# HGRN: the first growth of the keys moved from VectorE to GpSimd

## The chip, the cores and the metric
One core of a Trainium2 chip runs the whole kernel in one launch. The metric is the time of the device in microseconds (us). TensorE multiplies, VectorE and ScalarE do the elementwise work on both memories (SBUF and the accumulators in PSUM), GpSimd does elementwise work on SBUF, and SyncE starts the DMAs.

## What is computed
The reference is one layer of a decoder, for a prompt of 512 tokens and eight samples of 8 tokens (576 tokens in all) with a model width of 1024, followed by a final RMSNorm. One projection feeds a sliding window attention and HGRN2, a recurrence of 8 heads with a 128x128 state each. Cut to that recurrence:

```python
def step(S, inp):
    qc, kc, vc, gc = inp
    b = jnp.cumsum(gc, axis=1)
    o_inter = jnp.einsum('bthk,bhkv->bthv', qc * jnp.exp(b), S)
    diff = b[:, :, None] - b[:, None, :]
    decay = jnp.where(tri, jnp.exp(jnp.where(tri, diff, 0.0)), 0.0)
    att = jnp.einsum('bthk,bshk,btshk->bhts', qc, kc, decay)
    o_intra = jnp.einsum('bhts,bshv->bthv', att, vc)
    b_last = b[:, -1]
    S = jnp.exp(b_last)[..., None] * S + jnp.einsum(
        'bshk,bshv->bhkv', kc * jnp.exp(b_last[:, None] - b), vc)
    return S, o_inter + o_intra
```

The decay between two tokens of a head is a product over the tokens between them, different for each of the 128 channels.

## The kernel before
Activations lie with the features on the 128 partitions and the 576 tokens along the columns. The big products run over weight units of 1 MB: a DMA brings a unit to `raw`, ScalarE copies it to `wR` (L1071), VectorE subtracts to get the rest that the copy lost (L1388, four instructions of 512 columns for a unit), and TensorE multiplies both parts (L832). Each engine has its own program. All of them follow one list of events, which the function `walk()` writes out, so the order of each engine's work is fixed. Into the tiles of the projection, between 318 and 600 us, `walk()` weaves the slots of HGRN: `hgrn_slots()` gives, for each head r (0 to 7) and each of the six levels l of `LEVELS = (0, 4, 8, 16, 32, 64)`, one event `g_level`, and beside it what remains of the head before (`g_keys`, `g_state`, `g_sample`, `g_out`, `g_norm`, `g_scale`) and what prepares the head after (`g_diff`, `g_exp`, `g_operands`).

The decayed scores of a head are built from small blocks to large ones. `g_exp` makes the decays inside each block of four tokens: `eD` holds the growth for each token and, in its last 144 columns, the one at the head of each block. `g_operands` makes the queries `qe` and the keys `ke` of the base level. At level 0 TensorE multiplies `ke` and `qe` (L934 and L935) and signals `s_lv`. VectorE then grows both operands, so that they hold the decay to the borders of the block of four, keeps the whole block's decay in `g`, clears `att`, and copies the scores into it under a mask (L1585, L1586). At a level l above 0 TensorE multiplies the grown operands (L941, and L944 for the samples), and VectorE grows the halves of each pair of blocks (L1572, L1573), multiplies neighbouring decays (L1574) and copies under a mask (L1590). The growth at level 0 is:

```python
if l == 0:
    head, tail = eD[:, TOK:].unsqueeze(2), blocks(eD, 4, TOK)[:, :, 3:4]
    done(dve.tensor_tensor(blocks(k, 4, TOK), blocks(k, 4, TOK), tail.to_broadcast([P, QUADS, 4]), ALU.mult))
    done(dve.tensor_tensor(blocks(q, 4, TOK), blocks(q, 4, TOK), head.to_broadcast([P, QUADS, 4]), ALU.mult))
    done(dve.tensor_tensor(G[r % 2][:, 0:QUADS].unsqueeze(2), head, tail, ALU.mult), signal)
```

These are L1564 (keys), L1565 (queries) and L1566 (the decay of the block). `done` raises a semaphore at the end of an instruction and makes the engine wait for it, so that an engine's instructions follow one another. L941 of level 1 waits for `s_op`, which L1566 raises, and for `s_pred`, which the masked copy L1586 raises. ScalarE's `g_exp` of the next head overwrites `eD`, and so waits for the `s_op` that L1566 of the head before raised.

GpSimd does only single subtractions and additions of 576 columns elsewhere: `hR` (L1710) and `rb` (L1696, L1704) around the norms, and `actR` (L1717) in the MLP. In the stage of HGRN it has no work.

Of the kernel before, what the change touches and what calls it, by code (L numbers as in the profile page):

```python
# [27 lines left out]
ALU = mybir.AluOpType  # L28
# [3 lines left out]
P = 128  # L32
# [5 lines left out]
TOK = SEQ + SMP  # L38
# [13 lines left out]
NL = len(LEVELS)  # L52
MASK = (NL - 1) * HALF + TOK
QUADS = TOK // 4
# [322 lines left out]
def program(nc, a, o):  # L377
# [5 lines left out]
    with ctx:  # L383
# [3 lines left out]
        def sem(name):  # L387
            return ctx.enter_context(nc.semaphore(name))
# [61 lines left out]
        QE, KE, ATT, G = [qe0, qe1], [ke0, ke1], [att0, att1], [g0, g1]  # L450
# [41 lines left out]
        s_pn, s_pt, s_ptc, s_pv, s_otc = (sem(n) for n in ("s_pn", "s_pt", "s_ptc", "s_pv", "s_otc"))  # L492
        s_kw = sem("s_kw")
        s_D, s_E, s_base, s_op, s_lv, s_pred = (sem(n) for n in ("s_D", "s_E", "s_base", "s_op", "s_lv", "s_pred"))
        s_hats = sem("s_hats")
        s_kt, s_ktc, s_ds, s_st, s_vb = sem("s_kt"), sem("s_ktc"), sem("s_ds"), sem("s_st"), sem("s_vb")
        s_dss, s_sn = sem("s_dss"), sem("s_sn")
        s_sic = sem("s_sic")
# [8 lines left out]
        def ordered(eng, own, start=None):  # L507

            seen = dict(start or {})

            def done(ins, s=None, by=1):
                s = own if s is None else s
                seen[s] = seen.get(s, 0) + by
                ins.then_inc(s, by)
                eng.wait_ge(s, seen[s])
            return done
# [5 lines left out]
        def square(k):  # L522

            return tmp[k % 4] if k else rb
# [26 lines left out]
        def blocks(t, m, w):  # L551

            return t[:, 0:w].rearrange("p (a m) -> p a m", m=m)

        def decay(r, m, w):

            return G[r % 2][:, DECAY[m]:DECAY[m] + w // m].rearrange("p (a two) -> p a two", two=2)

        def act_tile(x):

            n = 2 * x.i + x.n
            return (n // 4 % 2) * 4 + n % 4
# [144 lines left out]
        def _(pe):  # L707
# [215 lines left out]
            def g_level(r, l):  # L923

                n, m, q, k = r * NL + l, LEVELS[l], QE[r % 2], KE[r % 2]
                if l == 0:
                    pe.wait_ge(s_base, r + 1)
                    if n:
                        pe.wait_ge(s_pred, n)
                    else:  # L930
                        pe.wait_ge(s_kw, 2)
                    for c in range(TT):
                        cols = slice(c * P, (c + 1) * P)
                        pe.matmul(A[0][:, cols], k[:, cols], q[:, cols], start=True, stop=True)  # L934
                    pe.matmul(A[1][:, 0:SMP], k[:, SEQ:TOK + SMP], q[:, SEQ:TOK], start=True, stop=True).then_inc(s_lv, 1)  # L935
                    return
                bank = A[l % 2]
                pe.wait_ge(s_op, r * (NL - 1) + l)
                pe.wait_ge(s_pred, n if l == 1 else n - 1)
                for c in range(TT):  # L940
                    mm = pe.matmul(blocks(bank[:, c * HD:(c + 1) * HD], m, HD), k[:, c * P:(c + 1) * P],  # L941
                                   blocks(q[:, c * P:(c + 1) * P], 2 * m, P)[:, :, m:2 * m], start=True, stop=True)
                if m < NT:
                    mm = pe.matmul(blocks(bank[:, SEQ // 2:HALF], m, SMP // 2), k[:, SEQ:TOK + SMP],  # L944
                                   blocks(q[:, SEQ:TOK], 2 * m, SMP)[:, :, m:2 * m], start=True, stop=True)
                mm.then_inc(s_lv, 1)
# [106 lines left out]
        def _(act):  # L1053
            done = ordered(act, s_act, {s_hi: 4})
            seen = {"tanh": 0, "logs": False}

            def logs_and_exps():

                if not seen["logs"]:
                    act.preload_act_table_set("natural_log_exp_and_others")  # L1060
                seen["logs"] = True
# [158 lines left out]
            def g_exp(r):  # L1220

                act.wait_ge(s_D, r + 1)
                if r:
                    act.wait_ge(s_op, (r - 1) * (NL - 1) + 1)
                logs_and_exps()
                done(act.activation(eD[:], D[:], ACT.Exp))
                done(act.activation(D[:, 0:TOK], D[:, 0:TOK], ACT.Exp, scale=-1.0), s_E)
# [61 lines left out]
        def _(dve):  # L1289
            done = ordered(dve, s_dve)  # L1290
# [267 lines left out]
            def g_grow(r, l):  # L1558

                m, q, k = LEVELS[l], QE[r % 2], KE[r % 2]  # L1560
                signal = s_hats if l == NL - 1 else s_op
                if l == 0:
                    head, tail = eD[:, TOK:].unsqueeze(2), blocks(eD, 4, TOK)[:, :, 3:4]
                    done(dve.tensor_tensor(blocks(k, 4, TOK), blocks(k, 4, TOK), tail.to_broadcast([P, QUADS, 4]), ALU.mult))  # L1564
                    done(dve.tensor_tensor(blocks(q, 4, TOK), blocks(q, 4, TOK), head.to_broadcast([P, QUADS, 4]), ALU.mult))  # L1565
                    done(dve.tensor_tensor(G[r % 2][:, 0:QUADS].unsqueeze(2), head, tail, ALU.mult), signal)  # L1566
                    return
                w = TOK if m < NT else SEQ
                g = decay(r, m, w)
                shape = [P, w // (2 * m), m]  # L1570
                early, late_ = blocks(k, 2 * m, w)[:, :, 0:m], blocks(q, 2 * m, w)[:, :, m:2 * m]
                done(dve.tensor_tensor(early, early, g[:, :, 1:2].to_broadcast(shape), ALU.mult))  # L1572
                done(dve.tensor_tensor(late_, late_, g[:, :, 0:1].to_broadcast(shape), ALU.mult))  # L1573
                done(dve.tensor_tensor(G[r % 2][:, DECAY[2 * m]:DECAY[2 * m] + w // (2 * m)].unsqueeze(2), g[:, :, 0:1], g[:, :, 1:2], ALU.mult), signal)  # L1574

            def g_level(r, l):

                m, n, att = LEVELS[l], r * NL + l, ATT[r % 2]
                dve.wait_ge(s_lv, n + 1)
                g_grow(r, l)  # L1580
                if l == 0:
                    if r >= 2:
                        dve.wait_ge(s_ost, r - 1)
                    done(dve.memset(att[:], 0.0))
                    done(dve.copy_predicated(att[:, 0:SEQ], levels[:, 0:SEQ], A[0]))  # L1585
                    done(dve.copy_predicated(att[:, SEQ:TOK], levels[:, SEQ:TOK], A[1][:, 0:SMP]), s_pred)  # L1586
                    return
                w = TOK if m < NT else SEQ
                at = TOK + (l - 1) * HALF
                done(dve.copy_predicated(blocks(att, 2 * m, w)[:, :, m:2 * m], blocks(levels[:, at:at + HALF], m, w // 2), blocks(A[l % 2], m, w // 2)), s_pred)  # L1590
# [97 lines left out]
        @block.gpsimd  # L1688
        def _(pool):
            done = ordered(pool, s_pool)  # L1690

            def squares(n, k):

                if 0 < k <= SUMMED:
                    pool.wait_ge(s_sq, n * KT + k + 1)
                    done(pool.tensor_tensor(rb[:], rb[:], square(k)[:], ALU.add), s_acc)  # L1696

            def last_squares(j):

                x, k = FINAL[j], FINAL_K[j]  # L1700
                cols = FINAL_COLS[x.half]
                if 0 < k <= SUMMED:
                    pool.wait_ge(s_sq, 2 * KT + j + 1)
                    done(pool.tensor_tensor(rb[:, cols], rb[:, cols], square(k)[:, cols], ALU.add), s_acc)  # L1704

            def modulate(n, k0):
                for k in (k0, k0 + 1):
                    pool.wait_ge(s_hhi, n * KT + k + 1)
                    cols = slice(k * TOK, (k + 1) * TOK)
                    done(pool.tensor_tensor(hR[:, 1, cols], tmp[k % 4][:], hR[:, 0, cols].bitcast(F32), ALU.subtract), s_hlo)  # L1710

            def evac(x):
                if x.kind == "up":
                    n = 2 * x.i + x.n
                    pool.wait_ge(s_ahi, n + 1)
                    a_ = actR[:, act_tile(x)]
                    done(pool.tensor_tensor(a_[:, 1, :], tmp[n % 2][:], a_[:, 0, :].bitcast(F32), ALU.subtract), s_alo)  # L1717

            for ev, *x in walk():
                if ev == "norm":  # L1720
                    for k in range(KT):
                        squares(0, k)
                elif ev == "stats":
                    squares(*x)
                elif ev == "last_squares":
                    last_squares(*x)
                elif ev == "modulate":
                    modulate(*x)
                elif ev == "evac":
                    evac(*x)  # L1730

# [62 lines left out]
```

## Time and profile before

| what | value |
|---|---|
| median of the runs | 1154.33 us (1153.62 to 1155.26) |
| the profiled execution, its own time | 1155.09 us |
| its span, first to last instruction | 1153.3 us |
| TensorE busy | 1102.6 us (96%) |
| VectorE busy | 682.0 us (59%) |
| ScalarE busy | 487.1 us (42%) |
| GpSimd busy | 87.9 us (8%) |
| mean granted clock of TensorE | 0.984 |

In the rows, PE is TensorE's multiplication and PEld its weight load, DVE is VectorE, ACT ScalarE, POOL GpSimd, and L with a number is a line of the kernel. Times in a row are in us from the start of the span unless they are called ns. "[0.68 <-DVE att L1586]" means that the engine stood idle for 0.68 us before it, and that what ended the idle time was VectorE's instruction of that line, which wrote `att`.

### The profile page before, as it was taken

How to read it: one execution, taken by the hardware profiler on the slowest of the kernel's cores; microseconds unless marked ns; L12 is line 12 of the kernel's file. 1: busy time of each engine (PE TensorE's matmuls, PEld its weight loads, DVE VectorE, ACT ScalarE, POOL GpSimd, SP SyncE). 2: the span in 40 equal slices, each digit the busy share in tenths (PEclk: the TensorE clock that was granted, in tenths of full speed). 3: DMA queues.
4: the chain of work that ended last, by engine and by line, in shares of the span. 5: the costliest groups of instructions: out<-in, count | busy, mean ns of one | idle time of the engine just before them, and what ended most of it. 6: DMA issues, size and time to landing. Idle time of an engine off the chain costs nothing.

```text
span 1153.3 us, 21500 instructions
## 1 busy us (share of the span) xinstructions
PE 1102.6 (96%) x8725; PEld 1043.2 (90%) x8725; DVE 682.0 (59%) x1512; ACT 487.1 (42%) x851; POOL 87.9 (8%) x65
## 2 busy tenths in 40 slices
PE   5998999998999999999999998899999999999997
PEld 4797889886899999999899998899999999999997
DVE  5735554444377877778875545637354564636465
ACT  3533557466453454643354224533323323242334
POOL 2400000000000000000000011420101001010101
PEclk9899999998999999999999999999999999999998
DMA  9884333212321323221323371132232223223202
GB/s 302 278 300 146 111 111 97 88 38 73 119 93 56 97 74 113 77 76 50 100 77 94 133 259 56 50 98 74 74 110 74 74 74 105 79 74 93 74 17 83
DMA packets 108775, 120.20 MB, mean 104 GB/s; under 512 B 2692, under 2 KB 98780, under 8 KB 108389
## 3 DMA queue, kind: packets, MB, share of 16 engines
q1 hardware_dynamic: 108677, 118.83, 32.1%
q8 instruction: 69, 1.13, 0.4%
q14 instruction: 29, 0.24, 0.1%
HBM read 108.99 MB, written 11.80 MB: 105 GB/s over the span
## 4 chain that ended last, share of the span: by engine, by line
PE 79%; DVE 11%; ACT 5%; issue 3%; DMA 1%; POOL 0%; SPq 0%; DVEq 0%; ACTq 0%; POOLq 0%
PE PS L832 59%; PE PS L787 4%; PE PS L941 3%; DVE wR L1388 2%; PE PS L805 2%; PE PS L778 1%; DVE xhat L1356 1%; ACT wR L1071 1%; PE PS L911 1%; PE PS L889 1%; ACT pr L1198 1%; PE PS L875 1%; DMA xn<-in_x_sample 1%; PE PS L1002 1%; PE PS L754 1%
## 5 line engine op out<-in xcount | busy, mean ns | idle before, releaser
L832 PE MATMUL PS<-hR,wR 128*128 128x288 f32 x3744 | 523.7, 298 | 0.8 <-issue 0.8
L832 PEld LDWEIGHTS PS<-hR,wR 128*128 128x128 f32 x3744 | 503.0, 189 | 9.7 <-issue 8.8
L832 PE MATMUL PS<-actR,wR 128*128 128x288 f32 (+2 forms) x1920 | 260.8, 296 | 1.8 <-DVE actR L1530 1.8
L1388 DVE TENSOR_TENSOR wR<-raw,wR 128x512 fp32r<-128x512 f32 x260 | 203.1, 781 | 96.4 <-ACT wR L1071 88.8
L832 PEld LDWEIGHTS PS<-actR,wR 128*128 128x128 f32 x1920 | 257.0, 189 | 3.0 <-DVE actR L1530 2.0
L1071 ACT ACTIVATE wR<-raw 128x512 fp32r<-128x512 f32 x260 | 164.4, 632 | 142.7 <-PE PS L832 132.9
L1450 DVE CAST actR<-tmp 128x576 fp32r<-128x576 f32 x32 | 15.2, 476 | 125.8 <-ACT tmp L1182 125.8
L787 PE MATMUL PS<-wR,hR 128*128 128x256 f32 x600 | 77.5, 286 | 0.0
L787 PEld LDWEIGHTS PS<-wR,hR 128*128 128x128 f32 x600 | 73.4, 191 | 2.0 <-issue 1.7
L1405 DVE SCALAR_TENSOR_TENSOR xT<-PS,mods,xT 128x288 f32<-128x288 f32 x68 | 35.2, 518 | 62.9 <-PE PS L832 56.2
L1181 ACT ACTIVATE tmp<-PS 128x576 f32<-128x576 f32 x32 | 20.8, 652 | 120.0 <-PE PS L832 117.8
L1717 POOL TENSOR_TENSOR actR<-tmp,actR 128x576 fp32r<-128x576 f32 x32 | 46.5, 1453 | 304.6 <-DVE actR L1450 304.6
L1696 POOL TENSOR_TENSOR rb<-rb,tmp 128x576 f32<-128x576 f32 x8 | 11.4, 1424 | 651.1 <-ACT tmp L1089 650.8
L1174 ACT ACTIVATE tmp<-PS 128x576 f32<-128x576 f32 x32 | 20.8, 651 | 59.3 <-PE PS L832 49.1
L941 PE MATMUL PS<-qe,ke 128*128 128x64 f32 x320 | 40.3, 269 | 1.4 <-DVE att L1586 1.3
L941 PEld LDWEIGHTS PS<-qe,ke 128*128 128x128 f32 x320 | 39.5, 191 | 2.1 <-issue 1.7
L805 PE MATMUL PS<-hR,wR 128*128 128x288 f32 x192 | 32.3, 333 | 5.5 <-POOL hR L1710 5.5
L805 PEld LDWEIGHTS PS<-hR,wR 128*128 128x128 f32 x192 | 30.7, 222 | 6.7 <-issue 4.3
L1198 ACT ACTIVATE pr<-pr,small 128x257 f32<-128x257 f32 (+2 forms) x49 | 23.5, 479 | 31.3 <-DVE small L1488 30.3
L1406 DVE SCALAR_TENSOR_TENSOR xT<-PS,mods,xT 128x224 f32<-128x224 f32 x68 | 30.7, 451 | 2.4
L1572 DVE TENSOR_TENSOR ke<-ke,g 128x256 f32<-128x256 f32 (+1 forms) x40 | 17.3, 432 | 18.8 <-PE PS L941 12.9
L1710 POOL TENSOR_TENSOR hR<-tmp,hR 128x576 fp32r<-128x576 f32 x16 | 24.0, 1497 | 50.2 <-ACT hR L1140 49.8
(219 smaller groups left out, 1070.2 us busy)
## 6 DMA issues: line engine op xcount, KB each, us to landing
raw<-in_w_in SPq DMA_DIRECT2D x30, 1024.0 KB, 5.2
raw<-in_w_up SPq DMA_DIRECT2D x16, 1024.0 KB, 5.4
raw<-in_w_down SPq DMA_DIRECT2D x16, 1024.0 KB, 5.0
mid<-in_w_ada SPq DMA_DIRECT2D x12, 1024.0 KB, 5.2
ada<-in_w_ada SPq DMA_DIRECT2D x8, 1024.0 KB, 12.5
S<-in_state_hgrn SPq DMA_DIRECT2D x8, 512.0 KB, 4.4
out_hgrn_sample<-S SPq DMA_DIRECT2D x8, 512.0 KB, 6.6
raw<-in_w_out SPq DMA_DIRECT2D x4, 1024.0 KB, 5.7
```

The lines of the kernel that those rows point to most:

```text
L787: mm = pe.matmul(PS[:, b0_, 0:UC], lhs[l], weights(x, w, k, 0, UC), start=(k == 0 and n == 0), stop=(k == KT - 1 and n == 2))
L805: mm = pe.matmul(PS[:, 2 * ((x.pair + m) % 2) + h, 0:HALF], weights(x, w, k, m * P), rhs, start=(k == 0 and n == 0), stop=(k == KT - 1 and ...
L832: mm = pe.matmul(PS[:, 2 * x.pair + h, 0:size], weights(x, w, k, col), rhs[r], start=(k == 0 and n == 0), stop=(k == last and n == 2))
L941: mm = pe.matmul(blocks(bank[:, c * HD:(c + 1) * HD], m, HD), k[:, c * P:(c + 1) * P], blocks(q[:, c * P:(c + 1) * P], 2 * m, P)[:, :, m:2 ...
L1071: done(act.activation(wR[split_index(n)][:, 0, cols], raw[SLOT[u]][:, cols], ACT.Copy), s_hi)
L1174: done(act.activation(halves(tmp[2 + n % 2][:]), src, ACT.Tanh, scale=0.5), s)
L1198: done(act.activation(t, t, ACT.Exp, scale=-1.0, bias=m[:, 0, e:e + 1], accum_out=m[:, 1, e:e + 1]), s_exp if e == heads - 1 else None)
L1388: done(dve.tensor_tensor(w[:, 1, cols], raw[SLOT[SPLITS[n]]][:, cols], w[:, 0, cols].bitcast(F32), ALU.subtract), s_lo)
L1405: done(dve.scalar_tensor_tensor(xT[:, m, 0:HALF], PS[:, b0_, 0:HALF], mods[:, gate + m, 0:1], xT[:, m, 0:HALF], ALU.mult, ALU.add))
L1406: done(dve.scalar_tensor_tensor(xT[:, m, HALF:SEQ], PS[:, b0_ + 1, 0:cut], mods[:, gate + m, 0:1], xT[:, m, HALF:SEQ], ALU.mult, ALU.add))
L1710: done(pool.tensor_tensor(hR[:, 1, cols], tmp[k % 4][:], hR[:, 0, cols].bitcast(F32), ALU.subtract), s_hlo)
L1717: done(pool.tensor_tensor(a_[:, 1, :], tmp[n % 2][:], a_[:, 0, :].bitcast(F32), ALU.subtract), s_alo)
```

## The change
At level 0 the multiplication of the keys is done by GpSimd, which waits for the same product of TensorE as VectorE does, and raises a new semaphore `s_kgrown`. The queries and the block's decay stay with VectorE. TensorE's and VectorE's level 1 wait for `s_kgrown` as well, and so does ScalarE before it overwrites `eD`.

```diff
@@ TensorE, g_level
                 pe.wait_ge(s_op, r * (NL - 1) + l)
+                if l == 1:
+                    pe.wait_ge(s_kgrown, r + 1)
                 pe.wait_ge(s_pred, n if l == 1 else n - 1)
@@ ScalarE, g_exp
                 if r:
                     act.wait_ge(s_op, (r - 1) * (NL - 1) + 1)
+                    act.wait_ge(s_kgrown, r)
@@ VectorE, g_grow
                 if l == 0:
                     head, tail = eD[:, TOK:].unsqueeze(2), blocks(eD, 4, TOK)[:, :, 3:4]
-                    done(dve.tensor_tensor(blocks(k, 4, TOK), blocks(k, 4, TOK), tail.to_broadcast([P, QUADS, 4]), ALU.mult))
                     done(dve.tensor_tensor(blocks(q, 4, TOK), blocks(q, 4, TOK), head.to_broadcast([P, QUADS, 4]), ALU.mult))
                     done(dve.tensor_tensor(G[r % 2][:, 0:QUADS].unsqueeze(2), head, tail, ALU.mult), signal)
                     return
+                if l == 1:
+                    dve.wait_ge(s_kgrown, r + 1)
@@ GpSimd
+            def g_level(r, l):
+
+                if l == 0:
+                    k = KE[r % 2]
+                    pool.wait_ge(s_lv, r * NL + 1)
+                    done(pool.tensor_tensor(blocks(k, 4, TOK), blocks(k, 4, TOK), blocks(eD, 4, TOK)[:, :, 3:4].to_broadcast([P, QUADS, 4]), ALU.mult), s_kgrown)
+
...
+                elif ev == "g_level":
+                    g_level(*x)
```

## Rows read from the trace of the kernel before

**Rows 1.** The page: busy time of each engine, and the chain by engine

```profile
PE 1102.6 (96%) x8725; PEld 1043.2 (90%) x8725; DVE 682.0 (59%) x1512; ACT 487.1 (42%) x851; POOL 87.9 (8%) x65
...
PE 79%; DVE 11%; ACT 5%; issue 3%; DMA 1%; POOL 0%; SPq 0%; DVEq 0%; ACTq 0%; POOLq 0%
```

**Rows 2.** Busy time by engine in the HGRN stage, 318 to 600 us

```profile
318.00:600.00 282.00, 276.65 (x2141) 261.58 (x2140) 217.26 (x454) 131.57 (x197) 0.00 (x0) 0.99 0.28 83
```

**Rows 3.** TensorE's waits, 318 to 600 us: total, times, longest

```profile
PE PS L934 <- DVE att L1590: 2.2, 1, 2.2
PE PS L941 <- DVE att L1586: 1.3, 2, 0.7
```

**Rows 4.** Timeline of head 3's level 0: start, length, instruction

```profile
421.55 0.33 PE L935 MATMUL PS<-qe,ke 128*128 128x64 f32 x2
...
421.99 0.76 DVE L1564 TENSOR_TENSOR ke<-ke,eD 128x576 f32<-128x576 f32 x1 [1.13 <-PE PS L935]
...
422.78 0.76 DVE L1565 TENSOR_TENSOR qe<-qe,eD 128x576 f32<-128x576 f32 x1
...
423.57 0.42 DVE L1566 TENSOR_TENSOR g<-eD 128x144 f32<-128x144 f32 x1
...
425.53 0.23 DVE L1586 COPY_PREDICATED att<-levels,PS 128x64 f32<-128x64 uint8 x1
...
425.91 1.08 PE L941 MATMUL PS<-qe,ke 128*128 128x64 f32 x8
```

**Rows 5.** Timeline, end of level 0 in heads 0, 2, 5, 7

```profile
326.74 1.08 PE L941 MATMUL PS<-qe,ke 128*128 128x64 f32 x8 [0.68 <-DVE att L1586]
...
390.36 0.23 DVE L1586 COPY_PREDICATED att<-levels,PS 128x64 f32<-128x64 uint8 x1
390.96 1.00 PE L941 MATMUL PS<-qe,ke 128*128 128x64 f32 x8
...
495.81 1.08 PE L941 MATMUL PS<-qe,ke 128*128 128x64 f32 x8 [0.62 <-DVE att L1586]
...
568.69 0.23 DVE L1586 COPY_PREDICATED att<-levels,PS 128x64 f32<-128x64 uint8 x1
570.35 1.00 PE L941 MATMUL PS<-qe,ke 128*128 128x64 f32 x8
```

**Rows 6.** VectorE's groups by shape, 318 to 600 us: busy us, mean ns

```profile
L1555 DVE TENSOR_TENSOR qe<-qs,eD 128x576 f32<-128x576 f32 x8 | 6.1, 758 | 0.3
L1564 DVE TENSOR_TENSOR ke<-ke,eD 128x576 f32<-128x576 f32 x8 | 6.1, 758 | 4.0 <-PE PS L935 3.8
...
L1566 DVE TENSOR_TENSOR g<-eD 128x144 f32<-128x144 f32 x8 | 3.4, 420 | 0.3
...
L1572 DVE TENSOR_TENSOR ke<-ke,g 128x256 f32<-128x256 f32 x32 | 13.6, 425 | 13.7 <-PE PS L941 12.9
```

**Rows 7.** GpSimd's groups by shape, whole span

```profile
L1696 POOL TENSOR_TENSOR rb<-rb,tmp 128x576 f32<-128x576 f32 x8 | 11.4, 1424 | 651.1 <-ACT tmp L1089 650.8
...
L1704 POOL TENSOR_TENSOR rb<-rb,tmp 128x256 f32<-128x256 f32 x1 | 0.7, 740 | 0.1
```

**Rows 8.** Timeline in the MLP: weight subtractions beside a GpSimd product, and alone

```profile
742.96 3.99 DVE L1388 TENSOR_TENSOR wR<-raw,wR 128x512 fp32r<-128x512 f32 x4
...
743.07 1.87 POOL L1717 TENSOR_TENSOR actR<-tmp,actR 128x576 fp32r<-128x576 f32 x1 [0.47 <-DVE actR L1450]
...
754.96 1.44 POOL L1717 TENSOR_TENSOR actR<-tmp,actR 128x576 fp32r<-128x576 f32 x1 [4.93 <-DVE actR L1450]
...
755.02 4.10 DVE L1388 TENSOR_TENSOR wR<-raw,wR 128x512 fp32r<-128x512 f32 x4 [0.20 <-ACT wR L1071]
...
1060.72 2.87 DVE L1388 TENSOR_TENSOR wR<-raw,wR 128x512 fp32r<-128x512 f32 x4
```

**Rows 9.** Stretches: length, busy by engine, granted clock, DMA share, GB/s

```profile
318.00:320.00 2.00, 1.04 (x9) 0.81 (x8) 1.83 (x5) 1.92 (x4) 0.00 (x0) 1.00 0.00 0
...
562.00:568.00 6.00, 6.00 (x42) 4.86 (x41) 5.54 (x10) 1.90 (x4) 0.00 (x0) 0.72 0.27 80
```

More of the change, by code:

```diff
@@ L494, in program @@
         s_D, s_E, s_base, s_op, s_lv, s_pred = (sem(n) for n in ("s_D", "s_E", "s_base", "s_op", "s_lv", "s_pred"))
-        s_hats = sem("s_hats")
+        s_hats, s_kgrown = sem("s_hats"), sem("s_kgrown")
         s_kt, s_ktc, s_ds, s_st, s_vb = sem("s_kt"), sem("s_ktc"), sem("s_ds"), sem("s_st"), sem("s_vb")
```

## The prediction

> **What bounds the kernel now.** I read the page first, for which engine has no room. TensorE is busy for 1102.6 us of 1153.3, GpSimd for 87.9, and 79% of the chain that ended last is TensorE's [rows 1]. So time taken off VectorE is worth only the TensorE idle time that it ends. The changed operation lies in the HGRN stage, between 318 and 600 us; there TensorE is busy for 276.65 us of 282.00, so 5.35 us is all that could be won, and GpSimd does nothing at all in it [rows 2]. The list of TensorE's waits in that stage says whose the idle time is: 1.3 us in two waits of L941 for `att` (L1586, the last instruction of level 0 on VectorE), and 2.2 us in one wait of L934 for `att` (L1590, level 5) [rows 3]. The 2.2 us wait comes at 561.68, at a head's change, behind three ACT activations and the operations that VectorE does on them; no level 0 lies in the chain from there back to TensorE's own work at 551, so the change does not touch it. What it can touch are the two waits for L1586.
>
> **The order inside level 0.** In head 3 VectorE grows the keys (421.99, 0.76 us), then the queries (422.78), forms the decay product (423.57), clears `att`, and copies twice under a mask, the last at 425.53 for 0.23 us; TensorE's next product of HGRN, L941, begins at 425.91 [rows 4]. That is 0.15 us after `att` is written (425.91 - 425.76), and in the two heads with a visible wait the same 0.15 us separates them; I take it as signal and start-up. So head 3 waits for nothing visible but has no slack either. By the same reading, start of L941 less the end of L1586 less 0.15, head 2 has 0.22 us (390.96 - 390.59 - 0.15; heads 4 and 6 repeat it within 0.04) and head 7 1.28 (570.35 - 568.92 - 0.15); head 1 is like head 7, with more. Heads 0 and 5 wait already, 0.68 and 0.62 us [rows 5].
>
> **What goes.** One VectorE instruction of 758 ns in each of 8 heads (L1564) [rows 6], with the gap behind it 0.79 us (422.78 - 421.99) [rows 4]. If nothing else happened, VectorE would be 0.79 us earlier at L1586 in every head.
>
> **What comes.** The same product as one GpSimd instruction over 128x576. GpSimd has done no product of this view in the kernel. On plain views of this size it takes 1424 ns, and 740 ns over 256 columns [rows 7], which is 2.14 ns per column and 0.19 us fixed. Lower end: if the decay, repeated over four columns, were fetched once, 144 columns stand in for 576 on one of two inputs, and 0.19 + 1.23 x 720/1152 is 0.96 us. Upper end: VectorE pays for a stepped view. Its product L1566 over 144 columns, one in four taken, costs 420 ns, where 757 ns for 576 and 425 ns for 256 columns (1.04 ns each, 0.16 fixed) give 0.31; the ratio is 1.35, and 1.43 x 1.35 is 1.94 us [rows 6]. VectorE's own growth with the repeated operand takes 758 ns, the same as its plain product L1555 [rows 6], so I take 1.43 us, between the 1424 ns and the 1.44 us of a product that goes first [rows 7, 8], and keep 0.96 and 1.94. By itself that length would cost nothing: begun at the signal of level 0 or 0.8 us later, the keys would be done over 1.5 us ahead of the masked copies that L941 waits for anyway.
>
> **What it does to VectorE.** This is where I think the gain goes. Later in the kernel GpSimd and VectorE do work side by side. Four weight subtractions of L1388 take 2.87 us where GpSimd is idle; with a GpSimd product that starts 0.11 us behind them (743.07) they take 3.99, and with one that starts 0.06 us ahead (754.96) 4.10 [rows 8]. So VectorE loses 1.12 or 1.23 us, most of GpSimd's 1.44, and the GpSimd product that comes second is itself longer (1.87 us). They take turns. L1388 works on two SBUF tensors; so do the query growth and the decay product. The Trainium skill ("SBUF — State Buffer", Who interferes with whom) gives this as a rule: a VectorE instruction with two SBUF inputs and a GpSimd instruction that reads SBUF shut each other out for the whole length of one of them. By that rule this trace agrees, 1.12 to 1.23 us lost to a 1.44 us product, and it speaks against this change.
>
> In the changed head both engines are released by the same signal of L935. VectorE starts 0.11 us after such an end (421.88 to 421.99) [rows 4], hardly longer than any start-up, and no row shows the two released together. I take the turn behind, as where VectorE has a queue it is already at work: queries, then GpSimd's 1.12 us, then the decay product. VectorE saves 0.79 and loses 1.12: it is 0.33 us **later** at L1586. (Turn ahead: 1.23 - 0.79 = 0.44.) In heads 0, 2, 5 and 7 VectorE still has weight subtractions in its queue when L935 ends; GpSimd then slips between those, and the loss is the same. Behind VectorE's late instructions stand the `vblk` product, weight subtractions and level 1; in the timeline the lateness meets idle time of VectorE, or slack of TensorE's next wait on it, before it costs more. Head 3 is the exception, where it runs on to L981, which already waits a little for `S`; TensorE comes there later by as much, so nothing is added.
>
> **The sum.** TensorE's delay is 0.33 less the slack: heads 0, 3 and 5 0.33 each, heads 2, 4 and 6 0.11 each, heads 1 and 7 nothing: 1.32 us. The extra semaphore waits (TensorE one a head, ACT and VectorE one a head) I cost at nothing: each is for a signal that came earlier than another that the same engine waits for at that place, and they cost a few hundredths where that cover is gone. No DMA is added or moved; GpSimd's next work is beyond 600 us. The profiled execution took 1155.09 us (span 1153.3), 0.76 above the median of the runs. 1155.09 + 1.32 is 1156.4, which is 1155.6 us on the scale of the median. With the turn ahead, 0.44: 3 x 0.44 + 3 x 0.22 = 1.98, or 1156.3. With GpSimd at 0.96 us VectorE loses 0.65, is 0.14 earlier, and TensorE wins 0.28: 1154.05. About 2.3 us (0.2%) is what can be told from no change here.
>
> **Rivals.**
> Slow product, slower by over 0.2%: GpSimd takes 1.94 us over the repeated, stepped operand. VectorE is late by 0.33 + 0.51 = 0.84, TensorE by 3 x 0.84 + 3 x 0.62 = 4.4 us: 1158.7. It decides from a product of about 1.60 us on (six heads, 0.17 each, on top of 1.32). For it: GpSimd has no row for such a view. Against it: VectorE's row of the same view is no slower than plain. The Trainium skill ("GPSIMD Engine Reference", Performance pitfalls for Q7 kernels) says that a GpSimd read stepping by more than 8 bytes costs about half again per element; the decay steps by 16 bytes from one block of four to the next, but not inside it, and no row here shows which counts. By that the product would be an estimated 2.0 us, and the time near that of this rival.
>
> No turns, the change does what it seems to: VectorE is 0.79 us earlier, the waits 0.68 and 0.62 go, nothing else does: 1154.33 - 1.30 = 1153.0, still within 0.2%. For it: only that these two particular instructions have not met before. Against it: both meetings in [rows 8].
>
> Clock: the longest wait in the stage, 2.2 us, is followed by six microseconds in which the granted clock averages 0.72 (1.2 GHz for part of them, 2.4 for the rest), 1.7 us lost, while the stretch from 318 to 320, in which TensorE also idles for 0.96 us, has 1.00 [rows 9]. In my forecast the waits of heads 0 and 5 become 1.0 us, like that harmless one. With the slow product they become 1.5; if both lose the clock it is 1158.7 + 3.4 = 1162.1.
>
> **Chances.** Forecast (product 1.43, turns, either order) 0.52, around 1155.6, its own range 1155.0 to 1156.6. Slow product 0.25; with lost clock 0.05 more. No turns 0.12. Cheap product 0.06. Slower by over 0.2% is then 0.30, and 0.01 for mishaps in the forecast's tail; faster by over 0.2% needs 2.3 us, more than the 1.3 us of waits that the change can reach, so 0.04 for what I do not see; within it 0.65. The range goes from the no-turns case, 1152.9, to just over the slow product, 1159.3; it leaves out the clock case and the tails.
>
> **What would show it.** VectorE's query growth or decay product about 1.1 us longer than 757 and 420 ns in each head; the new GpSimd instruction, 1.4 us if alone, up to 2.2 if it had to wait its turn; the wait of L941 for `att` up from 1.3 us in two heads to 2.6 in about six; the wait of L934 at 561 unchanged. If L1565 and L1566 stay at 757 and 420, the turns are wrong. If GpSimd needs over 1.6 us after its turn began, the size is wrong. If L941 waits for `ke` of GpSimd rather than for `att`, I have misread what is last.

## The result, and the profile after

The changed kernel was first timed in four executions: median 1161.52 us (1159.35 to 1162.88), beside 1154.72 (1153.62 to 1155.26) for the kernel before. The two medians lie 6.8 us apart; the ratio given with the result is 1.0047, 95% interval 1.0026 to 1.0068, which is 5.4 us slower (3.0 to 7.9). Three repeats of 11 or 12 executions each, beside 34 or 35 of before, gave 1.0031 (1.0018 to 1.0044), 1.0036 (1.0023 to 1.0049) and 1.0031 (1.0018 to 1.0045). All 35 together lie 3.5 us above before, give or take 0.5. So the change costs 3.5 us, where 1.3 were forecast.

The page of the changed kernel: busy time by engine, then two groups. They answer to [rows 1].

```profile
PE 1105.6 (95%) x8725; PEld 1045.9 (90%) x8725; DVE 684.6 (59%) x1504; ACT 487.2 (42%) x851; POOL 103.3 (9%) x73
...
L1721 POOL TENSOR_TENSOR ke<-ke,eD 128x576 f32<-128x576 f32 x8 | 15.5, 1935 | 501.0 <-PE PS L935 501.0
...
L943 PE MATMUL PS<-qe,ke 128*128 128x64 f32 x320 | 40.6, 270 | 2.3 <-DVE att L1590 2.2
```

VectorE has eight instructions fewer and is busy for 2.6 us more (682.0 before). L943 is before's L941, L1590 is L1586, L1567 and L1568 are the query growth and the decay product, and L1440 is L1437.

The groups of VectorE by shape, 318 to 606 us, the answer to [rows 6]:

```profile
L1568 DVE TENSOR_TENSOR g<-eD 128x144 f32<-128x144 f32 x8 | 8.9, 1112 | 0.3
...
L1440 DVE SCALAR_TENSOR_TENSOR xT<-tmp,xT 128x576 f32<-128x576 f32 x8 | 7.2, 900 | 4.8 <-ACT tmp L1176 4.6
L1567 DVE TENSOR_TENSOR qe<-qe,eD 128x576 f32<-128x576 f32 x8 | 7.2, 899 | 3.9 <-PE PS L935 3.8
```

The decay product, 420 ns before, takes 1112 ns in the mean. GpSimd holds it up in five heads; in head 5 it holds up the query growth instead, in head 0 one L1440 (a mean of 899 or 900 is seven of 758 ns and one of 1.88 us), and in head 7 a weight subtraction. The timeline shows how: first head 3, to be laid beside [rows 4].

```profile
424.95 0.76 DVE L1567 TENSOR_TENSOR qe<-qe,eD 128x576 f32<-128x576 f32 x1 [1.13 <-PE PS L935]
424.99 2.01 POOL L1721 TENSOR_TENSOR ke<-ke,eD 128x576 f32<-128x576 f32 x1 [33.33 <-PE PS L935]
...
425.74 1.54 DVE L1568 TENSOR_TENSOR g<-eD 128x144 f32<-128x144 f32 x1
...
428.82 0.23 DVE L1590 COPY_PREDICATED att<-levels,PS 128x64 f32<-128x64 uint8 x1
...
429.19 0.41 PE L943 MATMUL PS<-qe,ke 128*128 128x64 f32 x2 [0.25 <-DVE att L1590]
```

VectorE starts 0.04 us before GpSimd and goes first at 0.76 us. GpSimd follows, and is 2.01 us long because it has waited. Then the decay product, of 0.42, takes 1.54: 1.12 us lost, to the hundredth the loss in [rows 8]. From L1567's start to the end of L1590 it is 4.10 us; before, from L1564's start, 3.77. VectorE is 0.33 us later. In head 0 the turn falls on the operation ahead of the growth:

```profile
323.82 1.96 POOL L1721 TENSOR_TENSOR ke<-ke,eD 128x576 f32<-128x576 f32 x1 [271.47 <-PE PS L935]
...
324.51 1.89 DVE L1440 SCALAR_TENSOR_TENSOR xT<-tmp,xT 128x576 f32<-128x576 f32 x1
...
329.53 0.41 PE L943 MATMUL PS<-qe,ke 128*128 128x64 f32 x2 [1.02 <-DVE att L1590]
```

0.76 became 1.89, again 1.13, and TensorE's wait went from 0.68 to 1.02 us. The list of TensorE's waits, 318 to 606 us, the answer to [rows 3]:

```profile
PE PS L943 <- DVE att L1590: 2.2, 3, 1.0
PE PS L934 <- DVE att L1594: 2.2, 1, 2.2
```

The prediction named 2.6 us in about six heads. The list has three of them, heads 0, 3 and 5; the delays of heads 2, 4 and 6, 0.14 to 0.18 us each by TensorE's starts, are not in it.

Then the size of the loss in the stage. I take it between two products of TensorE, head 0's first L934 and the first L981 (now L983) behind 600 us. Before:

```profile
319.89 0.49 PE L934 MATMUL PS<-qe,ke 128*128 128x128 f32 x2 [0.96 <-DVE ke L1556]
...
608.33 1.13 PE L981 MATMUL PS<-vblk,khT 32*128 32x512 f32 x4
```

After:

```profile
322.35 0.49 PE L934 MATMUL PS<-qe,ke 128*128 128x128 f32 x2 [0.96 <-DVE ke L1559]
...
612.23 1.13 PE L983 MATMUL PS<-vblk,khT 32*128 32x512 f32 x4
```

288.44 us became 289.88: the stage lost 1.44 us, and 1.32 were forecast. But TensorE came to the stage 2.46 us later than before, through code that the edit does not touch, and the span is 5.8 us longer. The stage was foreseen and the whole was not; the experiments are mostly about that.

### The profile page after: what moved, and what is told of

It reads as the page before. It is cut to its first block, busy times and chain, and to the rows that moved or that the text cites. A ratio compares the mean times of both kernels' runs of the same rounds, so it can differ in the third digit from the quotient of the medians.

```text
span 1159.1 us, 21515 instructions
## 1 busy us (share of the span) xinstructions
PE 1105.6 (95%) x8725; PEld 1045.9 (90%) x8725; DVE 684.6 (59%) x1504; ACT 487.2 (42%) x851; POOL 103.3 (9%) x73
## 3 DMA queue, kind: packets, MB, share of 16 engines
q8 instruction: 69, 1.13, 0.4%
## 4 chain that ended last, share of the span: by engine, by line
PE 80%; DVE 11%; ACT 5%; issue 3%; DMA 1%; POOL 1%; SPq 0%; DVEq 0%; ACTq 0%; POOLq 0%
PE PS L832 58%; PE PS L787 4%; PE PS L943 3%; DVE wR L1391 2%; PE PS L805 2%; PE PS L778 1%; ACT wR L1073 1%; PE PS L911 1%; PE PS L889 1%; PE PS L875 1%; DVE xhat L1359 1%; ACT pr L1200 1%; DMA xn<-in_x_sample 1%; PE PS L1004 1%; PE PS L754 1%
## 5 line engine op out<-in xcount | busy, mean ns | idle before, releaser
L832 PE MATMUL PS<-hR,wR 128*128 128x288 f32 x3744 | 523.3, 297 | 0.8 <-issue 0.8
L832 PEld LDWEIGHTS PS<-hR,wR 128*128 128x128 f32 x3744 | 502.7, 188 | 9.8 <-issue 8.9
L832 PE MATMUL PS<-actR,wR 128*128 128x288 f32 (+2 forms) x1920 | 260.8, 296 | 1.8 <-DVE actR L1533 1.8
L832 PEld LDWEIGHTS PS<-actR,wR 128*128 128x128 f32 x1920 | 257.0, 189 | 3.0 <-DVE actR L1533 2.0
L1721 POOL TENSOR_TENSOR ke<-ke,eD 128x576 f32<-128x576 f32 x8 | 15.5, 1935 | 501.0 <-PE PS L935 501.0
L943 PE MATMUL PS<-qe,ke 128*128 128x64 f32 x320 | 40.6, 270 | 2.3 <-DVE att L1590 2.2
L943 PEld LDWEIGHTS PS<-qe,ke 128*128 128x128 f32 x320 | 39.4, 191 | 3.4 <-issue 2.8
```

The costliest lines, as they stand in the source:

```text
L832: mm = pe.matmul(PS[:, 2 * x.pair + h, 0:size], weights(x, w, k, col), rhs[r], start=(k == 0 and n == 0), stop=(k == last and n == 2))
```

## The experiments

Each was timed beside runs of before on the same chip. Two numbers are taken of each. **Stage** is the loss of TensorE from head 0's L934 to the product of L832 that before starts at 556.06 (heads 0 to 6), against before, from one trace. **Whole** is the mean time of the timed executions less that of before. Each execution's result also lists its mean granted clock; (1 - clock) x span is what stretches at 1.2 instead of 2.4 GHz would cost if TensorE were busy all through them. I call it **lost to the clock**, and **the rest** is the whole less it. The split is rough: the last 7 us of an execution, behind TensorE's last product, are mostly at 1.2 GHz (granted clock 0.53 in the trace of before, 0.50 in the first trace after) and count too, and so does time that TensorE would have waited anyway. Intervals are 1.96 standard errors.

**1. Control and repeats.** The kernel before, and the changed kernel, without an edit.

> The kernel before, unchanged, as a control. Every theory: ratio 1.000. What it tells is how far the stretches with TensorE's clock at half (30.7 us in all behind the start in the trace of before, in five places up to 734 us) stay where they were in another execution. If they stay within a few us of their places, the kernel before repeats them; if they wander, a single profile says little about them and the time of a run has this noise in it.

> The changed kernel, unchanged, for a tight ratio and a second trace. Theory A (turns of GpSimd and VectorE inside the HGRN stage cost 1.4 us; the other 4 us are clock falls outside it that came by chance): ratio towards 1.001 to 1.003, falls at other places than in the first trace of after. Theory B (the changed program has the falls for good): ratio 1.004 to 1.006 and falls again near 47, 109 and 740 us. In both, TensorE falls back by 1.3 to 1.6 us against before inside the HGRN stage, in heads 0, 2, 3, 4, 5 and 6.

> The changed kernel once more. Stage again 1.4 us slower than before. Whole time: with the first repeat it narrows the ratio; chance as the source of the rest predicts 1.0012 to 1.003, a lasting source predicts 1.003 to 1.004. Its trace gives a third set of places at which the clock falls.

Control: ratio 0.9998 (0.9985 to 1.0012), stage 0.00. But the single executions of before go from 1153.46 to 1161.11 us: the 1.6 us that its first four spanned were not its spread, and a single profile says little of the whole. The changed kernel: stage 1.43 and 1.49, steps of 0.30 to 0.34 us in heads 0, 3 and 5 and 0.15 to 0.18 in heads 2, 4 and 6; whole 3.7 and 3.5. The falls of the clock wander, also where no code differs. One is at 109 us in both repeats and in the first trace after, none in the control. Rows of stretches of 10 us there, control and then first placebo (below):

```profile
107.00:117.00 10.00, 7.86 (x74) 6.46 (x75) 4.91 (x21) 4.82 (x14) 0.00 (x0) 1.00 0.58 195
```

```profile
107.00:117.00 10.00, 7.41 (x59) 5.00 (x60) 3.71 (x16) 4.08 (x12) 0.00 (x0) 0.83 0.63 208
```

The granted clock, third number from the end, is 1.00 in one and 0.83 in the other, behind the same wait of 3.40 us.

**2. Placebo: the waits and a GpSimd instruction, but no turns.**

```diff
+                    done(dve.tensor_tensor(blocks(k, 4, TOK), blocks(k, 4, TOK), tail.to_broadcast([P, QUADS, 4]), ALU.mult))
                     done(dve.tensor_tensor(blocks(q, 4, TOK), blocks(q, 4, TOK), head.to_broadcast([P, QUADS, 4]), ALU.mult))
...
-                    done(pool.tensor_tensor(blocks(k, 4, TOK), blocks(k, 4, TOK), blocks(eD, 4, TOK)[:, :, 3:4].to_broadcast([P, QUADS, 4]), ALU.mult), s_kgrown)
+                    done(pool.memset(tmp_s[:], 0.0), s_kgrown)
```

> The keys stay on VectorE as in before; the new semaphore, all its waits and a GpSimd instruction in its place stay, but that instruction only clears a small scratch tile (64 columns, reads nothing). Theory A (turns): no delay of TensorE in the HGRN stage (under 0.2 us), VectorE's growth and decay product at 757 and 420 ns, ratio 1.000 within 0.001. Theory B (a program of another size or with more semaphore waits has its clock falls elsewhere): no delay in the stage either, but ratio 1.003 to 1.005 as in after, with the added stretches of half clock outside it. Rival C (the waits themselves cost): a delay in the stage of 0.1 us or more a head.

> The placebo again. If any change of the program costs, ratio 1.0005 to 1.0015 as in the first (1.0006); if that was chance, 1.000 within 0.0007. Stage within 0.2 us of before apart from clock falls.

Stage 0.00 in both, ratios 1.0006 (0.9990 to 1.0022) and 1.0003 (0.9988 to 1.0017). So in the stage neither the waits nor the added instruction cost anything; in the whole it is 0.3 us, give or take 1.1. Its groups are those of before:

```profile
L1567 DVE TENSOR_TENSOR ke<-ke,eD 128x576 f32<-128x576 f32 x8 | 6.1, 758 | 4.0 <-PE PS L935 3.8
...
L1569 DVE TENSOR_TENSOR g<-eD 128x144 f32<-128x144 f32 x8 | 3.4, 420 | 0.3
```

**3. The same GpSimd product, released later.** GpSimd waits for VectorE's decay product, so that it works beside the clearing and the masked copies.

```diff
-                    pool.wait_ge(s_lv, r * NL + 1)
+                    pool.wait_ge(s_op, r * (NL - 1) + 1)
```

> As after, but GpSimd waits for VectorE's decay product (the signal that level 1 waits for) instead of TensorE's level 0, so that it works beside the clearing of att and the masked copies, which have at most one SBUF tensor input. Theory of turns: VectorE's growth stays at 757 and its decay product at 420 ns, the GpSimd product takes 1.42 to 1.55 us and ends just before the last masked copy (1.7 us after its release), VectorE is 0.79 us earlier at L1590, and TensorE's waits of heads 0 and 5 (0.68 and 0.62 us) go: 1.3 us won in the stage against before. If masked copies also share the port: the copies are up to 1.2 us longer and the stage is 0.3 to 1.4 us slower than before. Whole time: 0.999 if the clock falls stay as in before, up to 1.003 if every changed program has the added ones.

> The late release once more. Stage again 2.0 us faster than before; whole time 0.998 if the stage alone decides, 0.9996 or more if moving TensorE earlier gives part back in the stages behind.

> The late release once more: stage 2.0 us faster than before, whole time 1.2 us faster by the first two (24 executions), so ratio 0.998 to 1.000.

Head 3 of the first one:

```profile
424.38 0.76 DVE L1567 TENSOR_TENSOR qe<-qe,eD 128x576 f32<-128x576 f32 x1 [1.13 <-PE PS L935]
...
425.17 0.43 DVE L1568 TENSOR_TENSOR g<-eD 128x144 f32<-128x144 f32 x1
...
425.74 1.44 POOL L1721 TENSOR_TENSOR ke<-ke,eD 128x576 f32<-128x576 f32 x1 [33.74 <-DVE g L1568]
425.78 0.54 DVE L1588 MEMSET att<- 128x576 f32 x1 [0.19 <-DVE g L1568]
...
426.36 0.75 DVE L1589 COPY_PREDICATED att<-levels,PS 128x512 f32<-128x512 uint8 x1
```

and its group over the stage:

```profile
L1721 POOL TENSOR_TENSOR ke<-ke,eD 128x576 f32<-128x576 f32 x8 | 11.6, 1446 | 504.6 <-DVE g L1568 504.6
```

The work is the same, and nobody is held up: decay product 0.43, clearing 0.54, masked copy 0.75 beside GpSimd, and GpSimd itself 1446 ns. So the repeated view costs GpSimd 0.02 us over a plain one ([rows 7]: 1424), and the extra half microsecond of the changed kernel (1935 ns) was waiting. Both waits of L943 for `att` are gone from the list. Stage: 2.00, 2.01 and 2.03 us **faster** than before, in all three. I had expected 1.3; head 0 and head 5 gave 0.77 and 0.78, more than their listed waits of 0.68 and 0.62, and head 3 gave 0.16 at L943 and 0.30 at L983, whose wait I had not counted. Whole: ratios 0.9996, 0.9985 and 0.9990, none clear by itself; together, 36 executions, 1.1 us faster, give or take 0.7. That is the version to keep of the two, though barely.

**4. The product left out.** Neither engine grows the keys at level 0; GpSimd clears the scratch tile. The keys of all later levels, the scores built of them and the states lack that factor.

```diff
-                    done(pool.tensor_tensor(blocks(k, 4, TOK), blocks(k, 4, TOK), blocks(eD, 4, TOK)[:, :, 3:4].to_broadcast([P, QUADS, 4]), ALU.mult), s_kgrown)
+                    done(pool.memset(tmp_s[:], 0.0), s_kgrown)
```

> The keys' growth is left out on both engines; GpSimd only clears a scratch tile, so nothing takes turns. It bounds what any move of this product off VectorE can win. Theory of turns: the same stage as with the late release, TensorE 2.0 us ahead of before (0.77 in head 0, 0.4 to 0.5 in head 3, 0.78 in head 5), growth at 757 and decay product at 420 ns. If the late release still loses something beside the masked copies, this one is ahead of it by that, 0.1 us or more. Whole time: ratio 0.998 to 0.999.

Stage 2.03 us faster, the same as with the late release to 0.03. So over heads 0 to 6 the late release wins all that taking the product off VectorE can win. Whole 1.7 us faster, give or take 1.5.

**5. Plain lateness, without GpSimd.** The kernel before, with short clears of a scratch tile on VectorE between the two growths (first (64, 64, 16) columns, then (64, 64)).

```diff
                     done(dve.tensor_tensor(blocks(k, 4, TOK), blocks(k, 4, TOK), tail.to_broadcast([P, QUADS, 4]), ALU.mult))
+                    for cols in (64, 64):
+                        done(dve.memset(tmp_s[:, 0:cols], 0.0))
```

> The kernel before with three short VectorE clears of a scratch tile (64, 64 and 16 columns, about 0.38 us with their gaps) at level 0 of each head: the same lateness of VectorE as in the changed kernel, without GpSimd and without any new wait. Theory A (only VectorE's lateness matters, by slack): stage 1.4 to 1.7 us slower than before, steps of 0.38 in heads 0, 3 and 5 and 0.16 in heads 2, 4, 6, as after. Whole time: if the change's whole time (3.1 us) is its stage's 1.4 us plus chance, this one is 1.001 to 1.002; if lateness at these places brings about clock falls elsewhere, it is 1.003, as after; if GpSimd's part outside the stage matters, 1.001.

> The kernel before with two short VectorE clears (64 columns each) at level 0, 0.33 to 0.40 us of lateness a head, as in the changed kernel, and no GpSimd. Stage 1.4 to 1.8 us slower. Whole: if lateness alone makes the whole 3.6 us (through falls of the clock), ratio 1.003; if GpSimd's part matters or the falls came by chance, 1.0012 to 1.002.

> The small plain delay once more (two VectorE clears of 64 columns, no GpSimd). If lateness alone brings the whole 3.5 us, 1.003; if it brings only the stage's loss, 1.0010 to 1.0020.

The first was larger than meant: steps of 0.52 us, stage 2.63, ratio 1.0034 (1.0018 to 1.0050), whole 3.8. The second and third give steps of 0.38 in heads 0, 3 and 5 and 0.22 to 0.24 in heads 2, 4 and 6, stage 1.81 and 1.78. The steps lie in the same six heads as in the changed kernel, and their size follows the lateness less the slack. TensorE's waits, 318 to 556 us, of the small delay and of the changed kernel:

```profile
PE PS L941 <- DVE att L1588: 2.4, 3, 1.1
```

```profile
PE PS L943 <- DVE att L1590: 2.2, 3, 1.0
```

But the whole of the small delay is 1.9 us, give or take 0.7 (ratios 1.0019 and 1.0020), though its stage loses more than that of the changed kernel with its 3.5.

**6. More traces, for the clock.**

> The kernel before, one more trace. Question: where do TensorE's clock falls lie ahead of the HGRN stage, where no program is changed? In its two traces there is none near 109 us, in seven of eight traces of changed programs there is one. If the falls there are chance, this trace and the next of before show one about every second time; if the edit brings them about, neither does.

> As the run before this one: chance predicts a fall near 109 us in one of the two, a cause in the edited program in neither.

> The changed kernel, a fourth trace. Stage 1.4 us slower than before by TensorE's starts. Ahead of the stage: if falls near 109 us belong to the changed program, it has one; by chance it may have none, as one of the two late-release traces.

> The placebo once more: stage within 0.2 us of before. A fall near 109 us if the form of the program brings it about; by chance in about every second trace.

> Control: ratio 1.000 within 0.001. One more trace of before: by chance its stage may lack the fall behind the wait of L934, as in two of four.

> The changed kernel against the same runs: ratio 1.003 again if the rest is lasting, stage 1.4 us slower apart from clock falls.

The first four of these are single executions. A fall near 109 us was in two of five traces of before, so that place does belong to chance. c5_before: ratio 0.9999 (0.9981 to 1.0016). The fall behind L934's wait of 2.2 us, which I had taken for a fixture ([rows 9]), was missing in two of five traces of before. The stretch of 10 us there, the first trace of before and then b3_before:

```profile
561.00:571.00 10.00, 9.32 (x66) 8.21 (x66) 8.80 (x15) 1.90 (x4) 0.00 (x0) 0.83 0.33 107
```

```profile
561.00:571.00 10.00, 8.34 (x69) 7.59 (x69) 9.29 (x17) 1.91 (x4) 0.00 (x0) 1.00 0.32 107
```

Without the fall TensorE is ahead at head 7, and that head's slack of 1.28 us is gone: in b3_before L1586 ends at 569.81 and L941 starts at 569.96. In a5_after, where the fall is missing too, head 7 waits:

```profile
573.15 1.08 PE L943 MATMUL PS<-qe,ke 128*128 128x64 f32 x8 [0.40 <-DVE att L1590]
```

From L934 to L983 a5_after needs 288.96 us, b3_before 287.24 to its L981: 1.72 us lost where no fall lies in the stage, against 1.44 where one does.

Over the timed executions (us, less before):

| kernel | executions | whole | lost to the clock | the rest | stage, traces |
|---|---|---|---|---|---|
| before again | 24 | 0.0 ± 0.9 | -0.2 ± 1.0 | 0.2 ± 0.8 | 0.0 |
| placebo | 24 | 0.3 ± 1.1 | 0.1 ± 1.2 | 0.3 ± 0.6 | 0.0 |
| changed | 35 | 3.5 ± 0.6 | 2.5 ± 0.8 | 0.9 ± 0.9 | 1.4 |
| small plain delay | 24 | 1.9 ± 0.8 | -1.0 ± 0.9 | 2.9 ± 1.0 | 1.8 |
| larger plain delay | 12 | 3.8 ± 1.6 | -0.6 ± 1.5 | 4.4 ± 1.1 | 2.6 |
| late release | 36 | -1.1 ± 0.7 | 1.8 ± 1.0 | -2.9 ± 0.8 | -2.0 |
| product left out | 12 | -1.7 ± 1.5 | 0.9 ± 1.9 | -2.6 ± 1.1 | -2.0 |

(Here the doubt of before's mean is in the intervals too.) The mean granted clock behind the third row is 0.9828, against 0.9850 for before. The rest doesn't match the stage in every row (4.4 beside 2.6, -2.9 beside -2.0), which shows how rough the split is. The whole less the stage needs no split: 2.1 us in the changed kernel, 0.1 in the small plain delay, 1.2 (± 1.6) in the larger, 0.9 in the late release, 0.3 in the placebo.

**7. The second modulation, in all twenty traces.** At 735 us of before TensorE waits for GpSimd's `hR`. The trace of the control, then c1_after:

```profile
731.11 1.44 POOL L1710 TENSOR_TENSOR hR<-tmp,hR 128x576 fp32r<-128x576 f32 x1 [1.00 <-ACT hR L1140]
```

```profile
734.64 1.43 POOL L1714 TENSOR_TENSOR hR<-tmp,hR 128x576 fp32r<-128x576 f32 x1 [1.33 <-ACT hR L1142]
```

and TensorE's waits at that place, again in that order:

```profile
PE PS L805 <- POOL hR L1710: 2.1, 2, 1.5
```

```profile
PE PS L805 <- POOL hR L1714: 2.1, 1, 2.1
```

GpSimd starts 0.33 us later against TensorE, a weight subtraction of VectorE beside it takes 1.69 us instead of 1.36, and two waits of 1.5 and 0.6 us become one of 2.1. The eight traces of before and of the plain delays have the two waits; the twelve of the changed kernel, placebo, late release and left out have the one. So it belongs to the added code and not to the product. The DMA queue that brings instructions has two packets there in c1_after (734 to 739.2) and none in the control (730.8 to 736): that the longer program loads its code at other places fits this, but no run tests it. Behind the one long wait the clock falls in six of the twelve traces; behind the two short ones it falls in none of eight.

## Why the prediction was wrong, by its steps

**Turns.** Right, and to the hundredth: 1.12 to 1.13 us lost in heads 0 and 3, VectorE 0.33 us later. The Trainium skill ("SBUF — State Buffer", Who interferes with whom) says that two SBUF inputs on VectorE exclude a reading GpSimd, and that VectorE instructions with at most one SBUF input don't (outside certain fast modes). Both halves hold here: the turns above, and in the late release VectorE's clearing and its long masked copy, at 0.54 and 0.75 us, unhindered beside GpSimd.

**GpSimd's duration.** Right: 1446 ns where it does not wait (the late release), 1.43 taken. The slow product is refuted, and with it the estimate from the Trainium skill ("GPSIMD Engine Reference", Performance pitfalls for Q7 kernels): a step of 16 bytes between blocks of four repeated reads did not bring 2.0 us. The section's remedy is a small inner step, which is 0 for the decay here, so it was my reading of its row that failed.

**No turns** is refuted by the groups, and the extra waits cost nothing in the stage, as the placebo shows.

**Slack.** Right in the main: 1.40 to 1.49 us over five traces, for 1.32. The small excess is in heads 2, 4 and 6 (0.14 to 0.18 each instead of 0.11). Head 7 was called safe with 1.28 us of slack, but that slack was the work of a clock fall just ahead of it, and in executions without the fall it costs about 0.3 us.

**The step that failed** is the sum's silent assumption that everything outside the six waits stays: 1155.09 + 1.32. It took the clock falls of one trace as fixed, put all work behind the stage at no change, and priced a changed clock only as a mishap of the slow product, at heads 0 and 5. In none of the five traces of the changed kernel is there a fall at those heads. Yet over 35 timed executions the whole lost 3.5 us (± 0.6) where the stage lost 1.4, and the lower granted clock (2.5 ± 0.8 us more lost to it) suggests that most of the missing 2.1 us are TensorE's clock.

One part can be placed. The second modulation has one TensorE wait of 2.1 us where before has two shorter ones (experiment 7), and behind it the clock falls, at 735 to 741 us, in three of five traces of the changed kernel, two of three of the late release, one of three placebos, and not in the one left out. Stretches of 15 us there, before and a5_after:

```profile
733.00:748.00 15.00, 12.05 (x88) 11.52 (x88) 9.20 (x13) 9.41 (x15) 6.12 (x4) 1.00 0.24 72
```

```profile
733.00:748.00 15.00, 12.01 (x79) 11.60 (x79) 8.15 (x15) 8.64 (x13) 6.14 (x4) 0.89 0.22 70
```

TensorE is busy for as long in both, and the granted clock is 1.00 and 0.89. From L983 (before's L981) to its last product TensorE needs 536.0 and 536.1 us in the changed kernel's two traces without that fall, and 538.3 to 539.4 in the three with it; in before it is 536.2 to 537.6. The means of five traces each differ by about 1 us. The wait comes with the added code, since the placebo has it too; that the fall behind it is more frequent with GpSimd's product than in the placebo is not shown by so few traces.

The remainder is open. Ahead of the stage, where the two kernels do the same work, TensorE comes 1.5 us later in the mean of five traces; but the three placebos come 2.3 later there, at a whole of 0.3, so that can be chance. Plain lateness of VectorE is not the cause by itself: the small plain delay, with more loss in the stage, has nothing beyond it (0.1 ± 0.8). A delay of just 1.4 us without GpSimd was not run, so it may still matter at which moment TensorE meets its later waits.

**What can be told from no change.** I said 0.2%. With before's executions spread over 7.6 us, four of them do not carry that; it took 35. The level was off as well: the sum stands on 1155.09 and 1154.33 us, and before's 104 executions beside the repeats average 1156.7. On 1154.33, the measured 3.5 gives 1157.8; the first four's 1161.5 is in part the draw.

## What to carry to other kernels

Before an operation goes from VectorE to GpSimd, look at what VectorE does beside it: on two SBUF tensors it is held up by most of GpSimd's duration, 1.12 of 1.44 us here, so a move that saves 0.79 ends 0.33 behind. Release it instead where VectorE clears, or copies from PSUM: the same product then held up nothing and won 2.0 us in the stage (1.1 ± 0.7 in the whole). Look at the waits behind the changed stage too, since added code can rearrange them. And where a kernel has waits that the clock follows, compare stretches of traces for the mechanism, and many executions for the whole.

## What the runs showed of the hardware that was not expected

The same program, with the same waits to 0.01 us, has or has not a stretch of 1.2 GHz behind a TensorE wait of 2.2 us (562, missing in two of five traces) or of 3.4 us (109, present in two of five). Single executions of one kernel differ by up to 7.6 us of 1157; such falls, at these and other places, have a part in it, and how large a part was not taken. A fall need not cost its face value: the one at 109 us made TensorE 1.5 us later (b3_before beside before), but the one at 562, 1.7 us by the clock, made the stage only 1.20 us longer (288.44 against 287.24), since part of it is time that head 7 would have waited.

Added code that does next to nothing in the stage (the placebo) made a GpSimd instruction start 0.33 us later some 170 us behind it, and two waits of TensorE became one; all twelve traces with the added code show it, and none of the eight without.

GpSimd's elementwise product takes 1446 ns over 576 columns with one operand repeated four times, against 1424 plain. A VectorE clear of 64 columns cost 0.19 us with its gap when two followed a growth, where I had reckoned 0.13.
